# Prelude order, score waits, PSUM banks and gather order in a two-layer decoder kernel

## What is computed

```python
cond = silu(c)
for l in range(2):
    mod = cond @ w_mod[l] + b_mod[l]                  # 6 vectors: shift, scale, gate, twice
    h = rms_norm(x, g_mix_pre[l]) * (1 + sc_mix) + sh_mix
    y = hybrid_mixer(h)                               # one projection, 8 stick-breaking heads,
                                                      # 8 softmax heads with relative bias,
                                                      # two branches gated by sigmoid, w_out
    x = x + gt_mix * rms_norm(y, g_mix_post[l])
    h = rms_norm(x, g_ffn_pre[l]) * (1 + sc_ffn) + sh_ffn
    y = swiglu(h) if l == 0 else moe_swiglu(h)        # dense; top 2 of 8 experts
    x = x + gt_ffn * rms_norm(y, g_ffn_post[l])
```

## Time and profile before

| | |
|---|---|
| median of three runs | 1797.66 us (1797.58 to 1798.4) |
| profiled execution | 1799.94 us |
| its span, first to last instruction | 1798.2 us |
| TensorE matmul, busy | 1669.9 us |
| VectorE busy | 1388.5 us |
| ScalarE busy | 1109.2 us |
| GpSimd (POOL) busy | 64.9 us |
| mean granted TensorE clock | 0.977 of full |
| moved by DMA | 512.05 MB, mean 285 GB/s |

### The profile page before, as it was taken

One profiled execution on the slowest core, in us unless ns is written; L12 is line 12 of the kernel. 1 busy time (PEld: TensorE's weight loads), 2 busy tenths in 40 slices (PEclk: granted clock), 3 DMA queues, 4 the chain that ended last, 5 costly groups with the idle time before them and its releaser, 6 DMA issues.

```text
span 1798.2 us, 23115 instructions
## 1 busy us (share of the span) xinstructions
PE 1669.9 (93%) x8014; PEld 1373.0 (76%) x8014; DVE 1388.5 (77%) x1258; ACT 1109.2 (62%) x966; POOL 64.9 (4%) x194
## 2 busy tenths in 40 slices
PE   4989979999979999699999999999999999999996
PEld 4967757777769777578878788788788788788785
DVE  5946867777776456668888978888888888788888
ACT  3555443333335554367777777777777777778775
POOL 0010010000000100410000000000000000000000
PEclk9999989999989999699999999999999999999998
DMA  8954646667648334069989989889899799899894
GB/s 332 374 196 167 234 164 259 248 265 280 247 154 325 118 110 171 24 242 370 368 312 375 353 315 365 334 345 364 306 375 378 294 364 374 305 366 367 316 373 163
DMA packets 72878, 512.05 MB, mean 285 GB/s; under 512 B 9011, under 2 KB 10236, under 8 KB 10876
## 3 DMA queue, kind: packets, MB, share of 16 engines
q1 hardware_dynamic: 71184, 510.18, 74.8%
q10 hardware_dynamic: 1644, 1.22, 0.2%
HBM read 510.30 MB, written 1.06 MB: 284 GB/s over the span
## 4 chain that ended last, share of the span: by engine, by line
PE 81%; DVE 8%; ACT 5%; issue 3%; POOL 2%; DMA 1%; ACTq 0%; DVEq 0%; POOLq 0%
PE ps L1215 25%; PE ps L1217 24%; PE ps L1216 24%; DVE wlo L290 4%; ACT whi L285 3%; PE ps L1438 2%; PE ps L1547 1%; DVE raw L299 1%; DMA qk<-in_rel_bias 1%; PE ps L1305 1%; PE ps L1236 1%; DVE x L773 1%; ACT vals L621 1%; ACT L285 0%; PE ps L1571 0%
## 5 line engine op out<-in xcount | busy, mean ns | idle before, releaser
L290 DVE TENSOR_TENSOR wlo<-raw,whi 128x2048 fp32r<-128x2048 f32 x436 | 993.5, 2290 | 251.1 <-ACT whi L285 249.2
L285 ACT ACTIVATE whi<-raw 128x2048 fp32r<-128x2048 f32 x436 | 833.3, 1915 | 294.4 <-PE ps L1217 294.2
L1215 PE MATMUL ps<-whi,hhi 128*128 128x512 f32 x1376 | 549.6, 399 | 13.2 <-DVE wlo L290 4.8
L1216 PE MATMUL ps<-whi,hlo 128*128 128x512 f32 x1376 | 540.2, 393 | 0.0
L1217 PE MATMUL ps<-wlo,hhi 128*128 128x512 f32 x1376 | 539.4, 392 | 0.0
L1215 PEld LDWEIGHTS ps<-whi,hhi 128*128 128x128 f32 x1376 | 261.0, 190 | 80.0 <-DVE wlo L290 13.7
L1217 PEld LDWEIGHTS ps<-wlo,hhi 128*128 128x128 f32 x1376 | 260.6, 189 | 56.0
L1216 PEld LDWEIGHTS ps<-whi,hlo 128*128 128x128 f32 x1376 | 261.0, 190 | 52.6 <-issue 1.0
L1215 PE MATMUL ps<-whi,ohi 128*128 128x512 f32 x624 | 249.6, 400 | 2.6 <-DVE wide L894 1.7
L1217 PE MATMUL ps<-wlo,ohi 128*128 128x512 f32 x624 | 243.8, 391 | 0.0
L1216 PE MATMUL ps<-whi,olo 128*128 128x512 f32 x624 | 243.1, 390 | 0.0
(11 more groups left out here) (209 smaller groups left out, 1091.6 us busy)
## 6 DMA issues: line engine op xcount, KB each, us to landing
raw<-in_w_moe SPq DMA_DIRECT2D x336, 1024.0 KB, 6.5
raw<-in_w_pre_moe SPq DMA_DIRECT2D x100, 1024.0 KB, 4.9
raw<-in_w_mod_units SPq DMA_DIRECT2D x48, 1024.0 KB, 5.3
x<-in_x ACTq DMA_DIRECT2D x1, 1024.0 KB, 9.5
bias<-dist_scratch SPq DMA_DIRECT2D x1, 1024.0 KB, 8.3
out<-x SPq DMA_DIRECT2D x2, 512.0 KB, 2.7
condb<-in_c SPq DMA_DIRECT2D x1, 512.0 KB, 5.4
qk<-in_bucket_onehot ACTq DMA_DIRECT2D x1, 49.4 KB
```

Of the source, the lines that this page charges most:

```text
L285: nc.scalar.activation(whi[:, s % SPLIT, :], raw[:, slot(s), :], ACT.Copy).then_inc(hi_done, 1)
L290: nc.vector.tensor_tensor(wlo[:, s % SPLIT, :], raw[:, slot(s), :], whi[:, s % SPLIT, :].bitcast(F32), ALU.subtract).then_inc(lo_done, 1)
L1215: nc.tensor.matmul(out, a_hi, b_hi, start=first, stop=False, **kw)
L1216: nc.tensor.matmul(out, a_lo, b_hi, start=False, stop=False, **kw)
```

## The change

It has five parts. **Prelude loads**: x is loaded first on SP's queue instead of first on ScalarE's; the four gain vectors come as one array in one DMA instead of four; the router's weights move from ScalarE's queue to SP's, at ring position 24. **Prelude work**: the squares of the second token half move to VectorE, with a semaphore of their own; ScalarE splits unit 0 between the second and third copy of transposed x; VectorE does `mod_columns(1)` in step 0 ahead of `hlo`, and from then on those of step k+2 after `split_lo(k)`. **Scores**: `scores(p)` waits for the attention matrix of pair p-2. **Dense block**: the transposes of token half c use bank 6 + c, so that the second no longer waits for `olo` of the first; `dense_down` of block 3 waits for the gate copy out of bank 7. **Experts**: both gather halves, and both `expert_tokens`, stand ahead of the transposes of `hid` and of their copy.

```diff
+            sp.dma_start(x[:], x_d.rearrange("b (c p) n -> p (b c) n", p=P)).then_inc(x_in, 16)
             sp.dma_start(condb[:], bass.AP(c_d.tensor, 0, [[0, P], [1, D]])).then_inc(cond_in, 16)
...
+                if pos == 24:
+                    sp.dma_start(wr[:], w_router[0].rearrange("(k p) e -> p k e", p=P)).then_inc(wr_in, 16)
...
-                act.wait_ge(sq_done, C)
-                for i in range(4):
+                act.wait_ge(sq_done, 1)
+                act.wait_ge(sq1_done, 1)
+
+                def x_transposed(i):
                     c, half = divmod(i, 2)
                     act.wait_ge(xT_done, i + 1)
                     nc.scalar.activation(h32[:, 4 * half:4 * half + 4, c * P:(c + 1) * P],
                                          bank[i].rearrange("p (k t) -> p k t", k=4), ACT.Copy).then_inc(xT_sb, 1)
+
+                for i in range(2):
+                    x_transposed(i)
+                split_hi(act, 0)
+                for i in range(2, 4):
+                    x_transposed(i)
...
-                    if k == 0:
-                        split_hi(act, k)
...
-            act.dma_start(x[:], x_d.rearrange("b (c p) n -> p (b c) n", p=P)).then_inc(x_in, 16)
             act.dma_start(rowsM, b_mod.rearrange("l (m p) -> (l m) p", p=P)).then_inc(small_in, 16)
-            for i, g in enumerate([g_mix_pre, g_mix_post, g_ffn_pre, g_ffn_post]):
-                act.dma_start(rowsB[16 * i:16 * i + 16, :], g.rearrange("l (m p) -> (l m) p", p=P))\
-                    .then_inc(small_in, 16)
+            act.dma_start(rowsB, g_rows).then_inc(small_in, 16)
...
-            act.dma_start(wr[:], w_router[0].rearrange("(k p) e -> p k e", p=P)).then_inc(wr_in, 16)
+            act.wait_ge(x_in, 16)
+            nc.scalar.activation(h32[:].rearrange("p k t -> p (k t)")[:, 0:D], x[:, 0, :], ACT.Square,
+                                 accum_out=ss[:, 0:1]).then_inc(sq_done, 1)
...
-            squares_of_x(0)
...
+                expert_tokens(i + 1, 1)
                 ffn_ghi(1, i * FBLK, 0, hidden_half(0))
-                expert_tokens(i + 1, 1)
...
+                mod_columns(dve, 0)
                 for k in range(KC):
-                    mod_columns(dve, k)
                     dve.wait_ge(mod_done, 2 * k + 2)
...
                     dve.wait_ge(ab_done, k + 1)
+                    if k == 0:
+                        mod_columns(dve, 1)
                     dve.wait_ge(xT_sb, 4)
...
                     split_lo(dve, k)
+                    for i in range(k + 2, min(k + 3, KC)):
+                        mod_columns(dve, i)
...
+            dve.wait_ge(x_in, 16)
+            nc.vector.scalar_tensor_tensor(h32[:].rearrange("p k t -> p (k t)")[:, D:2 * D], x[:, 1, :], 1.0, x[:, 1, :],
+                                           ALU.mult, ALU.mult, accum_out=ss[:, 1:2]).then_inc(sq1_done, 1)
             dve.wait_ge(cols_ps, 2)
...
-                        if p or l:
-                            pe.wait_ge(at_done, 16 * l + 2 * p)
+                        wait_at_least(pe, at_done, 16 * l + 2 * (p - 1))
...
-                wait_at_least(pe, gl_done, t * n + (base_of[n] + c))
+                wait_at_least(pe, gl_done, t * n + (base_of[n] + c - (n - 1)))
                 for k in range(4):
-                    ins = nc.tensor.transpose(bank[6][:, k * P:(k + 1) * P], hid[:, c, k * P:(k + 1) * P], ident[:])
+                    ins = nc.tensor.transpose(bank[6 + c][:, k * P:(k + 1) * P], hid[:, c, k * P:(k + 1) * P], ident[:])
...
-            pe.wait_ge(small_in, 16 * 5)
+            pe.wait_ge(small_in, 16 * 2)
...
                     if j == 4:
+                        if t == 3:
+                            pe.wait_ge(gate_sb, 4)
                         dense_down(t, s0 + 4, 0, t)
...
                 gather(i + 1, 0)
+                gather(i + 1, 1)
                 hidden_T(1, i * FBLK, 0)
-                gather(i + 1, 1)
```

More of the change, by code:

```diff
@@ L89, with build @@
         MODS_AFTER[max(n for kind, n in RING[:_pos] if kind == "unit")].append(_n)
-def build(nc, x_d, c_d, mod_units, b_mod, g_mix_pre, g_mix_post, g_ffn_pre, g_ffn_post, pre_units,
+def build(nc, x_d, c_d, mod_units, b_mod, g_rows, pre_units,
           rel_bias, w_router, moe_units, onehot_d, dist_scratch, out_d):
@@ L177, in build @@
         mod_done = sem("mod_done")
+        sq1_done = sem("sq1_done")
         xT_sb = sem("xT_sb")
@@ L389, in squares_of_x @@
                         act.wait_ge(ysq_done, squares[0])
-                    elif c == 0:
-                        act.wait_ge(x_in, 16)
                     scr = h32[:].rearrange("p k t -> p (k t)")[:, c * D:(c + 1) * D]
@@ L415, in norm @@
                 act.wait_ge(ab_done, AB[q] + 1)
-                act.wait_ge(sq_done, C * (q + 1))
+                act.wait_ge(sq_done, C * q + 1)
                 for c in range(C):
@@ L561, in ffn_ghi @@
                 act.wait_ge(gT_done, t * n + (base_of[n] + c + 1))
-                nc.scalar.activation(ohi[:, half, c * P:(c + 1) * P], bank[6][:].rearrange("p (k t) -> p k t", k=4),
+                nc.scalar.activation(ohi[:, half, c * P:(c + 1) * P], bank[6 + c][:].rearrange("p (k t) -> p k t", k=4),
                                      ACT.Copy).then_inc(gh_done, 1)
             base_of = {2: FFN_BASE[0], 1: FFN_BASE[1]}
-            act.dma_start(x[:], x_d.rearrange("b (c p) n -> p (b c) n", p=P)).then_inc(x_in, 16)
             act.dma_start(rowsM, b_mod.rearrange("l (m p) -> (l m) p", p=P)).then_inc(small_in, 16)
-            for i, g in enumerate([g_mix_pre, g_mix_post, g_ffn_pre, g_ffn_post]):
-                act.dma_start(rowsB[16 * i:16 * i + 16, :], g.rearrange("l (m p) -> (l m) p", p=P))\
-                    .then_inc(small_in, 16)
+            act.dma_start(rowsB, g_rows).then_inc(small_in, 16)
             act.dma_start(onehot, onehot_d).then_inc(rel_in, 16)
@@ L723, in norm @@
                 normed(q)
-                dve.wait_ge(sq_done, C * (q + 1))
+                dve.wait_ge(sq_done, C * q + 1)
                 dve.wait_ge(ab_done, AB[q] + 1)
@@ L880, in ffn_glo @@
                 dve.wait_ge(gh_done, t * n + (base_of[n] + c + 1))
-                nc.vector.tensor_tensor(olo[:, half, c * P:(c + 1) * P], bank[6][:].rearrange("p (k t) -> p k t", k=4),
+                nc.vector.tensor_tensor(olo[:, half, c * P:(c + 1) * P], bank[6 + c][:].rearrange("p (k t) -> p k t", k=4),
                                         ohi[:, half, c * P:(c + 1) * P].bitcast(F32), ALU.subtract)\
@@ L1106, in norm @@
                         pool.wait_ge(xn_done, C * q)
-                    inv_rms(rstd_done, sq_done, C * q + c + 1, c, 1, c)
+                    if q == 0 and c:
+                        inv_rms(rstd_done, sq1_done, 1, c, 1, c)
+                    else:
+                        inv_rms(rstd_done, sq_done, C * q + (c if q else 1), c, 1, c)
             def after(q, count):
@@ L1680, in _layout @@
     out = {"x": inputs["x"], "c": inputs["c"], "w_mod_units": mods}
-    out.update({k: inputs[k] for k in ("b_mod", "g_mix_pre", "g_mix_post", "g_ffn_pre", "g_ffn_post")})
+    out["b_mod"] = inputs["b_mod"]
+    out["g_rows"] = np.concatenate([inputs[k].reshape(-1, P) for k in ("g_mix_pre", "g_mix_post", "g_ffn_pre",
+                                                                     "g_ffn_post")])
     out["w_pre_moe"] = np.concatenate([mixers[0], dense, mixers[1]])
```

## The result

The changed kernel takes 1758.0 us (median; 1753.8 to 1759.0), the kernel before in the same series 1798.0. The ratio is 0.9772, with a 95% interval of 0.9754 to 0.9789: faster by 40.0 us, or 2.3%. The profiled execution took 1758.54 with a span of 1756.8, against 1799.94 and 1798.2 before, so span against span the gain is 41.4. I had forecast 43.4 as the sum and 1754.2 as the time.

What follows compares the result with a forecast made beforehand. TensorE, busy 93% of the span, was taken as the bound, so savings are its idle or lower-clock time. Terms 5.5 + 20.7 + 7.0 + 10.2 = 43.4 gave 1756.5, forecast 1754.2 for the median, range 1747 to 1765.7.

Steps and rivals of the forecast that it cites:

- Start: Before the first weight unit: first projection matmul 6.9 earlier, 1.4 given back, net 5.5 us (bounds 3 and 7.5).
- the give-back of 1.4: Start: column slot 4 slips 1.5 and one later slip follows, so wlo of units 4 to 6 comes late, 1.4 us.
- my other chain: Start: column slot 1 lands at 15.9, two column sums take 2.4 to 18.3, then hlo and wlo until 21.5.
- Router's weights: Load moved to SP's ring at position 24: five slots loaded ahead cover any delay, 0 us (bounds 0 and 3).
- Scores: 14 score sites: waits of 17.6 go, plus 1.4 overlap and 1.7 clock, 20.7 us (bounds 17.5 and 22.5).
- The 1.7 for the clock: Scores: time lost at the lower clock behind the longest wait, 3.12 at 108.00, returns, 1.7 us.
- Dense block: Second hidden transposes: 1.5 + 1.7 + 4.8, less 1.0 in block 3, 7.0 us (bounds 4 and 9).
- Experts: Both gathers before the hidden transposes: seven experts at 1.4, the first 0.4, 10.2 us (bounds 7.5 and 11.5).
- (a): Start bound by DMA: column slot 4 onward lands 3 or more late, 1 to 2 of 6.9 remain, about 1758; chance 0.13.
- (b): Scores: arguments wait for suffix-sum masks, 2 to 3 at up to half of 14 sites, about 1772; chance 0.07.
- (c): 28 sites: TensorE stops over 2 us at the next event, clock falls, 4.1 per site, slower; chance 0.02.
- (d): Whole kernel: freed waits were hidden, all terms nil but the score waits and these replaced, about 1797; chance 0.02.

Runs made afterwards that it cites:

- only_prelude: The start of the change alone (load order, gain vectors, squares, column slots, router weights) on the kernel before: 1791.9 us, ratio 0.9962.
- only_scores: Only the wait ahead of each pair of scores moved one pair back, on the kernel before: 1777.2 us, ratio 0.9879.
- only_experts: Only each expert's second gather ahead of the first hidden transpose, with ScalarE's copies in matching order, on the kernel before: 1789.7 us, ratio 0.9958.
- the fastest kernel: Changed kernel with block 3's gate wait later, VectorE making each expert's first hidden copy, and additions before the second hidden subtraction: 1749.1 us, ratio 0.9721.
- x_on_act: Changed kernel with x loaded first on ScalarE's queue again instead of SP's, rest of the new start kept: 1763.0 us, ratio 0.9813.

## Why the prediction was right, and where it was off

The sum was 43.4 and the measured gain 40.0, the forecast 1754.2 and the time 1758.0. The four stages are those that I named, each wait that I counted as removed is gone, and the parts add: timed alone they give 6.8 + 21.4 + 3.3 + 8.9 = 40.4.

- **Start, 5.5 against 7.5 (6.4 alone).** The first projection matmul came at 21.08 for a forecast of 21.5. The term that was mis-sized is the give-back of 1.4. Its mechanism is real, but it is a race of 1 to 2 us between column slot 4 and VectorE: of eight traces two show the wait of 1 (0.6 and 0.7 of it left at the first scores), the others none. And the chain that I had put at 17 with 1.3 to spare, small loads and transposed copies, is the bounding one in seven of the nine traces with the new order of column sums; with 8.79 behind the transposes it ended as late as my other chain, so the number came out right for a partly wrong reason. That x goes first is 6.4 of it.
- **Router's weights, 0.** Right. The load landed 7.9 behind its issue on SP's queue and nothing waited, where I had reckoned with up to 18.7. The statement of the Trainium skill on transfers under 512 B ("DMA: Bandwidth & Descriptors", Specifications) would bear on the load itself; that it held up the loads behind it is not seen here.
- **Scores, 20.7 against 20.1.** Right, term by term: all waits are gone, and the masks' reader comes late enough. The row of 3.28 shows that the masks were only covered, not made faster, and their reader comes 3.4 behind them there, where I had put 5 for masks at their usual speed. The shared port pair of the Trainium skill ("SBUF — State Buffer", Terms) still fits that row, and costs nothing now. The 1.7 for the clock belonged there in this profile, and in three of the four that have the wait of 3.1.
- **Dense block, 7.0 against 4.5.** Two terms failed. The additions cost 0.56 a block instead of 0.4 (5 blocks, 0.8 in all). And in block 3 the wait of 1.98 (2.1 forecast) brought the lower clock, 1.7, which I had only in my bounds. I had argued that waits of 1.5 cost no clock in the loop, which holds; one of 1.98 did in six of eight profiles. I had also counted 1.7 as returned behind the first transposes. The traces agree there, but three other kernels that keep those waits of 0.78 and 1.50 (only_prelude, only_scores, only_experts) have no fall behind them. That term came true by luck, since the one profile of before had the fall. The 3.3 of the part timed alone would fit that (4.6 less 1.7 are 2.9), but its interval of 1.3 to 7.6 does not decide it.
- **Experts, 10.2 against 8.8.** Right in mechanism, off by one step: I let ScalarE's second token copy start at the end of the first, at once. It needs the end of the second gather too, 0.28 later; and the first expert gave 0.33. 7 x 0.19 + 0.07 are the 1.4 of the difference. That would be some 0.2 of the 0.28 arriving at TensorE, which is my inference and not shown by a run of its own.
- **Rivals.** (a), the start bound by DMA: present as 1 us in two traces, never as 5. (b), the arguments waiting for masks: not seen. (c), new idle with clock falls: one site of 28, block 3. (d), that the waits were off the path: no, each part gave its gain alone.

## What to carry to other kernels

Where a wait is moved, move it to the first instruction that really needs it: one line placed one block of matmuls too early cost 3.9 of the change's gain, 2.0 as idle time and the rest as clock and lost overlap. A clock fall that stands in one profile is a chance, not a term: take it with the share of profiles in which it shows behind the same wait. And ask of each engine that follows a moved step what else its next instruction needs; in the experts the second input, the end of the second gather, is what I take to have kept 0.2 of the 1.4 back.

## What the hardware showed beyond that

- The granted clock behind one and the same wait differs between executions. Behind 3.10 to 3.12 ahead of the third scores it fell in three of four profiles; behind 1.98 in block 3 in six of eight; behind 0.78 and 1.50 at the first hidden transposes in one of four; behind 1.45 in the loop never. At these three sites each fall cost 1.7. From the first to the last instruction, TensorE spends 84.4 us at the lower level in the profile of before, 85.6 and 78.7 in the two of the changed kernel, and 74.5 to 90.3 over all fourteen. That is not a price list: the fastest kernel has 88.4, and x_on_act, whose span is 12.6 longer, has 74.5. In 16 to 24 us of that time TensorE is idle anyway. Over the 85 timed runs that have a mean granted clock beside their time, a run that lost 1 us more to the clock than its kernel's mean was only 0.33 us longer (correlation 0.65). So the falls make a part of the scatter of the medians, not all of it. Why a wait is followed by a fall in one execution and not in the next is open.
- The first loads land up to 0.9 apart from run to run (transposes of x at 12.13 to 13.08), and one column slot by 1.4 (33.6 and 35.0). A start that is cut this close to its loads varies by 1 us.
